# Layer norm of a gated convolution: statistics from transposed chunks in place of mean matmuls, and weight remainders that alternate between two engines

## The reference

```python
def layernorm(x, g, b):
    mu = jnp.mean(x, axis=-1, keepdims=True)
    var = jnp.mean(jnp.square(x - mu), axis=-1, keepdims=True)
    return (x - mu) * lax.rsqrt(var + EPS_LN) * g + b

def even_mixer(h, w_in, conv_w, conv_b, ln_g, ln_b, pool_w, pool_b, pool_scale, w_out):
    p = h @ w_in
    a_val, a_glu, a_gate, b_val, b_gate = split(p)
    u = a_val * sigmoid(a_glu)
    u = causal_depthwise_conv(u, conv_w, conv_b)     # 31 taps along the tokens
    u = silu(layernorm(u, ln_g, ln_b))               # over the 1024 channels
    ya = u * silu(a_gate)
    d = multiscale_pool_diff(b_val)
    yb = (group_matmul(d, pool_w) + pool_b) * pool_scale * silu(b_gate)
    return concat([ya, yb]) @ w_out                  # 2048 -> 1024, added to h
```

## Time and profile before

| what | value |
|---|---|
| device time, median of 3 runs | 1078.72 us (1078.23 to 1078.85) |
| the profiled execution | 1077.17 us, with a span of 1075.5 us from the first to the last instruction |
| mean granted TensorE clock | 0.995 of full speed |
| TensorE busy | 1030.2 us, 96% of the span, 7361 matmuls |
| VectorE / ScalarE / GpSimd busy | 62% / 57% / 55% |
| transfers | 159.55 MB, mean 148 GB/s |

### The profile page before, as it was taken

How to read it: one execution, slowest core, us unless ns; L and a number is a source line. 1 busy time by engine, 2 the same in 40 slices (tenths; PEclk the granted TensorE clock), 3 DMA queues, 4 the chain that set the end, 5 groups by cost and what they waited for, 6 DMA issues and landing times.

```text
span 1075.5 us, 19778 instructions
## 1 busy us (share of the span) xinstructions
PE 1030.2 (96%) x7361; PEld 934.0 (87%) x7361; DVE 669.6 (62%) x1438; ACT 613.8 (57%) x1241; POOL 591.7 (55%) x450
## 2 busy tenths in 40 slices
PE   9999999999999999999999999999899998899996
PEld 8799988898889998989989998878899986689885
DVE  7869577666664325696445544232699977568873
ACT  5455667766665447764446555354434456668953
POOL 3656345444444549745543444444778876568563
PEclk9999999999999999999999999999999999999998
DMA  8334333333333443235655656655455644544452
GB/s 312 97 118 151 107 117 101 116 119 114 101 101 119 145 139 100 89 99 194 203 185 167 187 182 191 192 173 178 149 163 159 188 153 143 202 132 137 145 171 97
DMA packets 43439, 159.55 MB, mean 148 GB/s; under 512 B 4944, under 2 KB 4944, under 8 KB 42832
## 3 DMA queue, kind: packets, MB, share of 16 engines
q1 hardware_dynamic: 43200, 158.25, 46.6%
q10 hardware_dynamic: 144, 0.03, 0.0%
HBM read 157.22 MB, written 1.05 MB: 147 GB/s over the span
## 4 chain that ended last, share of the span: by engine, by line
PE 72%; DVE 13%; ACT 6%; POOL 4%; issue 3%; DMA 1%; SPq 0%; DVEq 0%; ACTq 0%; POOLq 0%
PE p_proj L2015 15%; PE p_proj L2016 14%; PE p_proj L2017 14%; PE p_proj L1763 5%; PE p_proj L1764 4%; PE p_proj L1765 4%; PE p_score L1854 4%; POOL ring_lo L641 3%; PE p_proj L2000 3%; ACT ring_hi L1020 2%; PE p_pv L1882 2%; DVE ring_lo L641 2%; PE p_turn L1864 1%; DVE arena L1544 1%; PE p_score L1774 1%
## 5 line engine op out<-in xcount | busy, mean ns | idle before, releaser
L641 POOL TENSOR_TENSOR ring_lo<-ring,ring_hi 128x1024 fp32r<-128x1024 f32 x178 | 428.6, 2412 | 281.7 <-ACT ring_hi L1020 280.9
L2015 PE MATMUL p_proj<-arena_r,ring_hi 128*128 128x256 f32 x1664 | 497.1, 299 | 12.0 <-POOL ring_lo L641 5.9
L2016 PE MATMUL p_proj<-arena_r,ring_hi 128*128 128x256 f32 x1664 | 471.0, 283 | 0.0
L2017 PE MATMUL p_proj<-arena_r,ring_lo 128*128 128x256 f32 x1664 | 471.0, 283 | 0.0
L1020 ACT ACTIVATE ring_hi<-ring 128x1024 fp32r<-128x1024 f32 x276 | 289.9, 1054 | 123.2 <-PE p_proj L1765 65.3
L2015 PEld LDWEIGHTS p_proj<-arena_r,ring_hi 128*128 128x128 f32 x1664 | 319.1, 192 | 29.0 <-issue 18.1
L2016 PEld LDWEIGHTS p_proj<-arena_r,ring_hi 128*128 128x128 f32 x1664 | 319.2, 192 | 7.3 <-issue 6.0
L2017 PEld LDWEIGHTS p_proj<-arena_r,ring_lo 128*128 128x128 f32 x1664 | 319.0, 192 | 0.0
L641 DVE TENSOR_TENSOR ring_lo<-ring,ring_hi 128x1024 fp32r<-128x1024 f32 x98 | 130.0, 1326 | 107.0 <-ACT ring_hi L1020 105.6
L1763 PE MATMUL p_proj<-ring_hi,arena_r 128*128 128x512 f32 x272 | 108.1, 397 | 9.6 <-POOL ring_lo L641 7.1
L1765 PE MATMUL p_proj<-ring_lo,arena_r 128*128 128x512 f32 x272 | 106.1, 390 | 0.0
(11 more groups left out here) (324 smaller groups left out, 1301.6 us busy)
## 6 DMA issues: line engine op xcount, KB each, us to landing
ring<-w_stream SPq DMA_DIRECT2D x286, 512.0 KB, 3.6
arena<-w_tok SPq DMA_DIRECT2D x1, 1632.0 KB, 13.5
arena<-w_rgi SPq DMA_DIRECT2D x1, 1536.0 KB, 6.2
arena<-x_t SPq DMA_DIRECT2D x4, 256.0 KB, 6.8
arena<-w_cmp SPq DMA_DIRECT2D x1, 1024.0 KB, 16.4
sbuf_s<-x_tok SPq DMA_DIRECT2D x1, 1024.0 KB, 4.8
out_t<-arena SPq DMA_DIRECT2D x4, 256.0 KB, 2.7
kk_s<-g_rows SPq DMA_DIRECT2D x1, 512.0 KB, 5.7
```

Of the source, the lines that this page charges most:

```text
L641: return eng.tensor_tensor(ring_lo[:, u % RING, :, :].rearrange("p k n -> p (k n)"), ring[:, u % RING, :, :].rearrange("p k n -> p (k n)") ...
L2015: pe.matmul(slot(s)[:, 0:S], w_hi, hi, start=(c == 0), stop=False)
L2016: pe.matmul(slot(s)[:, 0:S], w_hi, lo, start=False, stop=False)
L2017: mm = pe.matmul(slot(s)[:, 0:S], w_lo, hi, start=False, stop=(c == n - 1))
```

## The change

- The mean and variance no longer come from matmuls with a constant matrix. TensorE transposes each pair of chunks (`lt`, four 128x128 transposes, tokens on the partitions) into a bank of PSUM; VectorE takes `bn_stats` of it (`lst`). Three pairs lie in the convolution, the fourth behind it.
- `lroot`: two `bn_aggr` on VectorE give mean and variance of each token, ScalarE takes the square root of 128x2 numbers (its tables for the root and for tanh are loaded by name ahead of it and behind it), VectorE inverts and makes the shift.
- `lz`: each pair is scaled and shifted per token, out of PSUM into `arena`, pairs 0 and 2 on ScalarE, 1 and 3 on VectorE. `lb` transposes back into the banks, where `lnout` reads.
- `lnout` has two activations a chunk on ScalarE, with gain and shift per channel, and two products on VectorE.
- `lns`, `lsq` and `lnv` go. The units of even_yb stand at other places among these steps, and `split ya` one chunk earlier.
- `on_gpsimd` no longer names even_yb, so its remainders alternate: the first, third, fifth and seventh are now VectorE's.

```diff
             if conv in (11, 19, 27):
-                out += [("lnm", conv // 8 * 2 - 2), ("lnm", conv // 8 * 2 - 1)]
+                out.append(("lt", conv // 8 - 1))
+            if conv in (13, 21, 29):
+                out.append(("lst", conv // 8 - 1))
...
-    out += sum(even_yb[0:3], []) + [("lnm", 6), ("lnm", 7)] + [("lns", c) for c in range(8)] + [("lsq", c) for c in range(8)]
-    out += even_yb[3] + [("lnv",)]
+    out += even_yb[0] + even_yb[1] + even_yb[2][0:1] + [("lt", 3), ("lst", 3), ("lroot",)] + even_yb[2][1:]
+    out += even_yb[3][0:2] + [("lz", b) for b in range(4)] + [("lb", 0), ("lb", 2)] + even_yb[4][0:1]
+    out += [("lb", 1), ("lb", 3)] + even_yb[3][2:] + even_yb[4][1:]
     for c in range(8):
-        out += (even_yb[4 + c // 3] if c % 3 == 0 else []) + [("lnout", c)]
-        if c >= 2:
-            out.append(("split", "ya", c - 2))
-    out += [("split", "ya", 6), ("split", "ya", 7)] + even_yb[7]
+        out += (even_yb[5 + c // 3] if c % 3 == 0 and c < 6 else []) + [("lnout", c)]
+        if c >= 1:
+            out.append(("split", "ya", c - 1))
+    out += [("split", "ya", 7)] + even_yb[7]
...
-            if unit_of[u] in ("br_dsa", "dq", "nq", "val_glu", "b_gate", "a_gate", "even_yb", "xr"):
+            if unit_of[u] in ("br_dsa", "dq", "nq", "val_glu", "b_gate", "a_gate", "xr"):
                 return True
...
+                elif k == "lroot":
+                    act.preload_act_table(ACT.Sqrt)
+                    act.wait_ge(sem("ln_var"), 1)
+                    act.activation(ln_rs, ln_mv[:, :, 1], ACT.Sqrt, bias=small[:, 1:2]).then_inc(sem("ln_root"), 1); note(sem("ln_root"))
+                    act.preload_act_table(ACT.Tanh)
+                elif k == "lz" and s[1] % 2 == 0:
+                    b = s[1]
+                    act.wait_ge(sem("ln_scale"), 2)
+                    for t in range(NT):
+                        ins = act.activation(A(AC + 2 * b + t), ln_bank(b)[:, S * t:S * t + S], ACT.Identity,
+                                             bias=ln_shift[:, t:t + 1], scale=ln_rs[:, t:t + 1])
+                    ins.then_inc(sem("lz_act"), 1); note(sem("lz_act"))
                 elif k == "lnout":
                     c = s[1]
-                    act.wait_ge(sem("ln_z"), c + 1)
+                    act.wait_ge(sem("lb_done"), 2 if c < 2 else 4)
                     if c >= 4:
                         act.wait_ge(sem("yaf_ready"), c - 3)
-                    act.activation(ln_gate(c), A(AC + c), ACT.Tanh, bias=half[:, 8 + c:9 + c], scale=2.0)\
+                    act.activation(A(AC + c), ln_gate(c), ACT.Identity, bias=half[:, 172 + c:173 + c], scale=half[:, c:c + 1])
+                    act.activation(ln_gate(c), ln_gate(c), ACT.Tanh, bias=half[:, 8 + c:9 + c], scale=half[:, 180 + c:181 + c])\
                         .then_inc(sem("ln_tanh"), 1); note(sem("ln_tanh"))
...
+                elif k == "lst":
+                    b = s[1]
+                    dve.wait_ge(sem("lt_done"), b + 1)
+                    for t in range(NT):
+                        ins = dve.bn_stats(ln_parts[:, t, b, :], ln_bank(b)[:, S * t:S * t + S])
+                    link(ins)
+                elif k == "lroot":
+                    for t in range(NT):
+                        ins = dve.bn_aggr(ln_mv[:, t, :], ln_parts[:, t, :, :].rearrange("p b n -> p (b n)"))
+                    ins.then_inc(sem("ln_var"), 1); note(sem("ln_var"))
+                    dve.wait_ge(sem("ln_root"), 1)
+                    link(dve.reciprocal(ln_rs, ln_rs))
...
+                elif k == "lt":
+                    b = s[1]
+                    pe.wait_ge(sem("econv_done"), 2 * b + 2)
+                    for t in range(NT):
+                        for m in range(2):
+                            at = S * t + P * m
+                            mm = pe.transpose(ln_bank(b)[:, at:at + P], A(AC + 2 * b + m)[:, P * t:P * t + P], ident[:, :])
+                    mm.then_inc(sem("lt_done"), 1)
+                elif k == "lb":
+                    b = s[1]
+                    pe.wait_ge(sem("lz_act"), 1 if b == 0 else 2)
+                    pe.wait_ge(sem("lz_dve"), 1 if b == 0 else 2)
+                    for t in range(NT):
+                        for m in range(2):
+                            mm = pe.transpose(ln_gate(2 * b + m)[:, P * t:P * t + P], A(AC + 2 * b + t)[:, P * m:P * m + P],
+                                              ident[:, :])
+                    mm.then_inc(sem("lb_done"), 1)
```

More of the change, by code:

```diff
@@ L405, in psum_tenants @@
             add("pv", s, "A")
-        elif k == "lns" and s[1] == 0:
-            add("mean", ("ln",), "D")
-        elif k == "lnv":
-            add("mean", s, "A")
     return where, turns
@@ L505, in program @@
         dec = sb("dec", [P, 32])
-        half = sb("half", [P, 180])
+        half = sb("half", [P, 188])
+        lnst = sb("lnst", [P, 60])
         m8 = sb("m8", [P, 8])
@@ L1625, in _ @@
                                 ins.then_inc(sem("econv_done"), 1); note(sem("econv_done"))
-                elif k == "lns":
-                    c = s[1]
-                    dve.tensor_tensor(A(AC + c), A(AC + c), take(("ln",)), ALU.subtract)\
-                        .then_inc(sem("lsub"), 1); note(sem("lsub"))
-                    if c == 7:
-                        settle()
-                        dve.nop().then_inc(read["mean", "D"], 1); note(read["mean", "D"])
-                elif k == "lnv":
-                    was_read(dve, s)
-                    link(dve.reciprocal(rin, root[:, 0, :]))
-                    for c in range(8):
-                        dve.scalar_tensor_tensor(out=A(AC + c), in0=A(AC + c), scalar=half[:, c:c + 1], in1=rin,
-                                                 op0=ALU.mult, op1=ALU.mult).then_inc(sem("ln_z"), 1); note(sem("ln_z"))
+                elif k == "lst":
[11 more added lines that the diff above has]
+                    for t in range(NT):
+                        dve.scalar_tensor_tensor(out=ln_shift[:, t:t + 1], in0=ln_mv[:, t, 0:1], scalar=small[:, 2:3],
+                                                 in1=ln_rs[:, t:t + 1], op0=ALU.mult, op1=ALU.mult)\
+                            .then_inc(sem("ln_scale"), 1); note(sem("ln_scale"))
+                elif k == "lz" and s[1] % 2 == 1:
+                    b = s[1]
+                    dve.wait_ge(sem("ln_scale"), 2)
+                    for t in range(NT):
+                        ins = dve.tensor_scalar(A(AC + 2 * b + t), ln_bank(b)[:, S * t:S * t + S], ln_rs[:, t:t + 1],
+                                                ln_shift[:, t:t + 1], ALU.mult, ALU.add)
+                    ins.then_inc(sem("lz_dve"), 1); note(sem("lz_dve"))
                 elif k == "lnout":
@@ L1643, in _ @@
                                                   op0=ALU.add, op1=ALU.mult))
-                    dve.scalar_tensor_tensor(out=A(SQ + c), in0=A(AC + c), scalar=half[:, 172 + c:173 + c],
-                                             in1=ln_gate(c), op0=ALU.add, op1=ALU.mult)\
+                    dve.tensor_tensor(A(SQ + c), A(AC + c), ln_gate(c), ALU.mult)\
                         .then_inc(sem("yaf_ready"), 1); note(sem("yaf_ready"))
```

31 lines of the change are left out of this document (7 added, 24 removed).

## The result

The changed kernel took 1083.20 us (median of 5 runs, 1080.09 to 1085.36) against 1078.74 us of the kernel before: a ratio of 1.0041, 95% interval 1.0027 to 1.0055. Run once more later it took 1081.94 us (ratio 1.0044, 1.0028 to 1.0059). The forecast was 1081.4. The profiled execution took 1082.54 us around a span of 1080.8, so the two traces lie 5.3 us apart.

What follows compares the result with a forecast made beforehand. TensorE, busy 96% of the span, was taken to bound the kernel. A later chain (+1.35 us) and a lower clock (+1.35 us) made +2.7 us on the median 1078.72: 1081.4, range 1076.8 to 1084.5.

Steps and rivals of the forecast that it cites:

- What follows hangs on TensorE's own results: From even_ya's second unit to the residual's transposes TensorE runs without a stop; what comes after depends on its results.
- the milestone I took: The start of even_ya's second unit on TensorE, at 921.50 before the change and forecast at 922.85.
- The chain, +1.35 us: From the convolution's last tap through layer norm and output chunks, even_ya's second unit starts at 922.85 instead of 921.50.
- The clock, +1.35 us: A TensorE rest of 5.3 us before even_ya's second token half halves the clock; bounds 0.75 to 3.5 us.
- Twice slow: Rival: the 3.0 us wait before even_yb's third unit also halves the clock, 1.8 us more, 1083.2; chance 0.12.
- No row shows it rise again: Claim that the profile shows the granted clock fall but never recover, so the clock's price has bounds only.
- what is late next is ScalarE with two activations: In the layer norm's output, ScalarE has no room from 907 on for two activations a chunk, 0.94 us.
- no more than a share of a gain: Rival: alternating even_yb's remainders does nothing, or is merely a share of the late-at-full-clock rival; no chance of its own.
- The lead is spent: TensorE's 0.84 us lead from the first new transposes is lost; the convolution's last tap ends near 891.87 as before.
- the full-clock case: Rival: even_ya's second unit is late but the clock stays up, only +1.35 us remains, 1080.1; chance 0.30.
- 0.75 with half of 1.37: Clock price before even_ya's second unit: lower end 0.75 us plus half of that unit's first six matmuls, taken as 1.35.

Runs made afterwards that it cites:

- e3: The changed kernel with matmuls of constants filling TensorE's rests before even_yb's third unit and even_ya's second token half: 1084.47 us, ratio 1.0048 to the kernel before.
- e1: The changed kernel with all of even_yb's remainders back on GpSimd, so the new layer norm alone: 1076.62 us, ratio 0.9988 to the kernel before.
- e4: The changed kernel with the first four chunks' output steps ahead of the steps of even_yb's sixth unit: 1079.15 us, ratio 1.0003 to the kernel before.
- e5: The changed kernel with only the remainder of even_yb's third unit back on GpSimd: 1082.81 us, ratio 1.0047 to the kernel before.

## Why the prediction was right, and where it wasn't

- **The place and the direction** held: TensorE's waits are those forecast, 2.96 us for "about 3.0" and 4.87 for 5.3; the eighth unit's wait is gone; ScalarE works the chunks from 907.55 to 918.04 (forecast 907 to 918.15); even_ya's second unit starts at 923.37 (922 to 924).
- **"What follows hangs on TensorE's own results"** failed: what follows hangs on w_rgi, 1.5 MB ahead of the weight stream on SyncE's queue. Its release is the end of even_ya's first unit, next to the milestone I took, so the sum was not hurt.
- **The chain, +1.35 us**, was +0.54 (e3's second half, 151.57 against 151.03, and the same at w_rgi). The terms behind it: statistics 0.76 a pair for 0.93, and 2.81 us from the start of the statistics to the end of the table load (897.49 to 900.30 in e3) for 3.15; a chunk's two activations 0.89 for 0.94, and all of them with splits and high half 10.5 for 11.1.
- **The clock, +1.35 us**, was 0.88 + 1.03 up to w_rgi. Both rests drew a fall; I had put the first into the rival "Twice slow" at 0.12, with 1.8 us: that is the course that the trace took, at half the price or less. "No row shows it rise again" was wrong: the trace of before has a fall and a rise near 116, behind a rest of 1.80 us, which I hadn't looked at:

```profile
116.00:117.00 1.00, 0.55 (x3) 0.56 (x4) 0.47 (x1) 0.95 (x6) 0.00 (x0) 0.76 0.00 0
117.00:119.00 2.00, 2.00 (x11) 2.00 (x11) 0.47 (x3) 1.91 (x7) 0.00 (x0) 0.50 0.00 0
119.00:120.00 1.00, 1.00 (x7) 1.00 (x7) 0.00 (x0) 0.99 (x3) 0.00 (x0) 0.53 0.00 0
```

- **The cause** was named too narrowly. I wrote that what is late next is ScalarE with two activations; e1 takes the loss away without touching ScalarE. The wait for the third unit was in my sum with 2.0 us, but I called the alternation worth no more than a share of a gain. It costs 3.4 us at w_rgi (155.17 against e1's 151.77). ScalarE's order wasn't innocent either: e4 leaves the alternation as it is, moves only the chunks' output steps ahead of the eighth unit's high half, and comes to 1079.15, a ratio of 1.0003. With the new layer norm either undoing alone takes the loss away.
- **"The lead is spent"** held: the last taps start 0.36 us earlier than before (117.23 against 117.59). Without the first unit's remainder on VectorE, 1.2 us of lead are left (e1, 116.40).
- **Luck.** Up to w_rgi the chain and the clock make 2.45 us (155.17 against 152.72) where I had 2.7, because the chain was 0.8 us too dear and the clock 0.6 us too cheap. The 2.8 us of falls in the odd mixer stood in no term, so the profiled execution came out at 1082.54 and not at 1079.9. Falls differ from run to run, and 1081.4 lies as near to the medians 1083.20 and 1081.94 as it does in part by luck.
- **Two slips in the sums.** The cheap end of the full-clock case is -0.25 (1.35 - 0.6 - 1.0), as its rival has it, and not -0.9, so the low end of the range would have been 1077.5. And 0.75 with half of 1.37 is 1.44, not 1.35. Neither bears on the outcome.

## What to carry to other kernels

Before an engine with free time takes over part of a stream, look at what stands behind the new instruction in its own queue: here two remainders of 1.24 us each between the last tap and the statistics, the first of which TensorE had to wait for, delayed two engines, though VectorE was busy for only 62% of the span before. Find the transfer that the next stage waits for, and what releases its issue; that, more than the next matmul, is where a stage's lateness is passed on. Undo each half of a change by itself before naming its cause: this one was a gain and a larger loss.

## What the runs showed that I had not expected

- The same rest of TensorE draws half clock in one execution and not in another: some 2.95 us did in four traces and did not in two, 1.80 us near 116 did in the trace of before and not in that of the changed kernel. The clock then stayed at half from 116.5 to 119.9 in the trace of before and from 893.9 to 897.3 in that of the changed kernel, and longer in some places; one of the long stretches, 914.5 to 921.3 in e1:

```profile
914.00:915.00 1.00, 0.00 (x0) 0.00 (x0) 0.64 (x3) 0.76 (x2) 0.34 (x1) 0.75 0.02 8
915.00:921.00 6.00, 3.83 (x9) 3.05 (x10) 5.11 (x6) 3.11 (x4) 2.37 (x1) 0.50 0.00 0
921.00:922.00 1.00, 1.00 (x5) 0.77 (x5) 0.00 (x0) 0.26 (x1) 0.67 (x1) 0.84 0.74 172
```

- A remainder on VectorE took 1.23 us alone, 2.47 beside one remainder of GpSimd (the one at 921.59 in the changed kernel) and 3.07 in e5.
